# Expert tiles of a mixture of experts: another order of transposes, and products that wait for one half of their operand at a time

## The reference

```python
for e in range(N_EXPERTS):
    h = jax.nn.silu(jnp.dot(xf, w_gate[e])) * jnp.dot(xf, w_up[e])
    y = y + combine[:, e:e + 1] * jnp.dot(h, w_down[e], preferred_element_type=jnp.float32)
```

## Time and profile before

| | |
|---|---|
| runs, us | 1010.88, 1011.61, 1014.06 |
| span of the profiled execution, first to last instruction, us | 1005.1 |
| around that span, against the median, us | 6.5 |
| PE busy, share of the span | 919.4 us, 91% |
| DVE busy | 616.7 us, 61% |
| ACT busy | 534.2 us, 53% |
| the expert tiles, first product of tile 0 to last product of tile 22 | 548.8 to 973.0 us |

### The profile page before, as it was taken

The page is one execution under the profiler, slowest core; times in us unless marked ns, Lnnn a source line. Parts: engine busy times, 40 slices in busy tenths (PEclk is TensorE's granted clock), DMA queues, the critical chain, the costliest instruction groups (busy, mean ns, idle before and its releaser), DMA issues.

```text
span 1005.1 us, 15974 instructions
## 1 busy us (share of the span) xinstructions
PE 919.4 (91%) x4959; PEld 744.9 (74%) x4960; DVE 616.7 (61%) x1182; ACT 534.2 (53%) x1008; POOL 177.8 (18%) x260
## 2 busy tenths in 40 slices
PE   5899999899989999989973999999999999999982
PEld 5777888687877788867742788888888888888850
DVE  5443644655744573465698989989456494564684
ACT  4343565542445565554343878877446584464460
POOL 4300002001000011100011234435222232221301
PEclk9998999989999999989975999999999999999996
DMA  8740114116342352310755999999868697674524
GB/s 252 120 108 22 42 43 130 61 43 201 115 104 84 112 183 54 116 42 22 281 215 171 352 362 394 389 374 392 275 203 260 197 342 228 218 248 116 150 107 193
DMA packets 95119, 183.95 MB, mean 183 GB/s; under 512 B 24064, under 2 KB 52975, under 8 KB 95072
## 3 DMA queue, kind: packets, MB, share of 16 engines
q1 hardware_dynamic: 80496, 137.91, 38.3%
q0 software_dynamic: 14144, 43.88, 16.4%
q10 hardware_dynamic: 432, 1.57, 0.4%
HBM read 159.85 MB, written 28.70 MB: 188 GB/s over the span
## 4 chain that ended last, share of the span: by engine, by line
PE 41%; DVE 15%; issue 6%; DMA 4%; ACT 3%; DVEq 1%; SPq 0%; ACTq 0%; POOL 0%; POOLq 0%
PE O L2009 9%; PE C L1728 7%; PE C L1730 7%; PE C L1729 7%; DVE split_main L1594 6%; PE O L1909 3%; PE T L1962 2%; PE S L1763 2%; PE T L1884 2%; PE S L1969 1%; PE T L1792 1%; DMA mixing<-in_w_out 1%; DMA mixing<-acc_dram 1%; ACT split_main L1092 1%; DVE mixing L1675 1%
## 5 line engine op out<-in xcount | busy, mean ns | idle before, releaser
L1594 DVE TENSOR_TENSOR split_main<-mixing,split_main 128x1024 fp32r<-128x1024 f32 x188 | 217.7, 1221 | 35.0 <-ACT split_main L1092 32.3
L1092 ACT CAST split_main<-mixing 128x1024 fp32r<-128x1024 f32 x188 | 186.4, 1050 | 17.2 <-PE C L1730 7.1
L1728 PE MATMUL C<-split_main,split_aux 128*128 128x512 f32 x368 | 143.9, 391 | 1.3 <-DVE split_aux L1600 1.3
L1730 PE MATMUL C<-split_main,split_aux 128*128 128x512 f32 x368 | 143.9, 391 | 0.0
L1729 PE MATMUL C<-split_main,split_aux 128*128 128x512 f32 x368 | 143.6, 390 | 0.0
L1728 PE MATMUL C<-split_main 128*128 128x512 f32 (+1 forms) x320 | 130.4, 407 | 3.5 <-DVE split_main L1434 3.0
L2009 PE MATMUL O<-split_main,split_aux 128*128 128x512 f32 x552 | 132.7, 396 | 0.0
L1729 PE MATMUL C<-split_main 128*128 128x512 f32 (+1 forms) x320 | 121.6, 380 | 0.0
L1730 PE MATMUL C<-split_main 128*128 128x512 f32 (+1 forms) x320 | 121.4, 379 | 0.0
L2009 PEld LDWEIGHTS O<-split_main,split_aux 128*128 128x128 f32 x552 | 100.2, 188 | 23.4 <-DVE split_aux L1615 4.7
L1728 PEld LDWEIGHTS C<-split_main,split_aux 128*128 128x128 f32 x368 | 69.5, 189 | 15.9 <-issue 1.5
(11 more groups left out here) (341 smaller groups left out, 1435.3 us busy)
## 6 DMA issues: line engine op xcount, KB each, us to landing
mixing<-in_w_down SPq DMA_DIRECT2D x64, 512.0 KB, 8.2
mixing<-in_w_gate SPq DMA_DIRECT2D x64, 512.0 KB, 9.1
mixing<-in_w_up SPq DMA_DIRECT2D x64, 512.0 KB, 6.1
mixing<-in_w_in SPq DMA_DIRECT2D x20, 512.0 KB, 3.8
mixing<-in_w_out SPq DMA_DIRECT2D x16, 512.0 KB, 4.1
mixing<-in_w_mem_kv SPq DMA_DIRECT2D x8, 512.0 KB, 6.1
mixing<-in_w_in SPq DMA_DIRECT2D x16, 256.0 KB, 3.7
x_dram<-x_nat POOLq DMA_DIRECT2D x8, 512.0 KB, 2.9
```

Source lines behind the costliest of these rows:

```text
L1092: nc.scalar.copy(wu[0][:, w, :], raw[:, w, :]).then_inc(unit_hi, 1)
L1594: nc.vector.tensor_tensor(wu[1][:, w, :], raw[:, w, :], wu[0][:, w, :].bitcast(F32), ALU.subtract).then_inc(unit_lo, 1)
L1728: ins = nc.tensor.matmul(out_ap, st[0], mvg[0], start=first, stop=False)
L1730: ins = nc.tensor.matmul(out_ap, st[1], mvg[0], start=False, stop=last)
```

## The change

In the first step of a tile, each unit's six products are issued as four with high halves of the rows, then two with low halves. PE waits for the high halves (`xgT_hi`) ahead of the tile, and for the low halves only ahead of the first product that reads them, the fifth. The transposes go in the order 4 row, 1 hidden, 4 row, 3 hidden. In the third step the units f = 0 and f = 1 wait for the high half of their part first and for the low half ahead of the fifth product; f = 2 and f = 3, which read the same part as f = 1, wait for neither. The products themselves are the same 72, and so are all other engines' programs.

```diff
                 with pe.Fori(lo, hi) as j:
-                    pe.wait_ge(xgT_lo, j + 1)
+                    pe.wait_ge(xgT_hi, j + 1)
                     for w in range(KD):
                         unit_wait(e, w)
-                        for k in range(2 * (w % 4), 2 * (w % 4) + 2):
-                            ins = three(Cb[w // 4][:, :], [xgT[0][:, k, :], xgT[1][:, k, :]],
-                                        [wu[b_][:, w, (k % 2) * 512:(k % 2 + 1) * 512] for b_ in range(2)],
-                                        k == 0, k == KD - 1)
+                        half, ks = Cb[w // 4][:, :], (2 * (w % 4), 2 * (w % 4) + 1)
+                        for part in range(2):
+                            for k in ks:
+                                nc.tensor.matmul(half, xgT[0][:, k, :], wu[part][:, w, (k % 2) * 512:(k % 2 + 1) * 512],
+                                                 start=(k == 0 and part == 0), stop=False)
+                        if w == 0:
+                            pe.wait_ge(xgT_lo, j + 1)
+                        for k in ks:
+                            ins = nc.tensor.matmul(half, xgT[1][:, k, :], wu[0][:, w, (k % 2) * 512:(k % 2 + 1) * 512],
+                                                   start=False, stop=(k == KD - 1))
                         ins.then_inc(units_used, 1)
-                    transpose_rows(j + 1, 0, 2)
+                    transpose_rows(j + 1, 0, 4)
                     transpose_h(j, 0)
-                    transpose_rows(j + 1, 2, KD)
+                    transpose_rows(j + 1, 4, KD)
                     transpose_h(j, 1)
                     pe.wait_ge(y_half[0], j + 1)
                     pe.wait_ge(y_half[1], j + 1)
                     for f in range(KF):
                         unit_wait(e, KD + f)
-                        pe.wait_ge(hT_lo, j * 2 + (f > 0) + 1)
                         st = [hT[0][:, f, :], hT[1][:, f, :]]
+                        if f < 2:
+                            pe.wait_ge(hT_hi, j * 2 + 2 + f + 1)
                         for a_, b_ in ((0, 0), (0, 1), (1, 0)):
+                            if a_ == 1 and f < 2:
+                                pe.wait_ge(hT_lo, j * 2 + f + 1)
                             for half in range(2):
```

## The result

The changed kernel took 1005.46 us (median of 18 runs) where the kernel before took 1010.47 (18 runs), 5.0 us less. Four of the 18 runs were disturbed, 1011.70 to 2756.90 us, and the comparisons leave such runs out: then the ratio is 0.9933, 95% interval 0.9908 to 0.9957, a gain of 6.8 us (4.3 to 9.3). Run twice more for this study, the same kernel gave 0.9971 (0.9948 to 0.9994) and 0.9958 (0.9925 to 0.9991). The mean of the three is 0.9954, some 4.7 us; the forecast was 5.0 of 1011.61, a ratio of 0.9951. All intervals hold the forecast's ratio, but the working has to be looked at apart from the sum, since the profiles show terms that were too large and others that were too small.

What follows compares the result with a forecast made beforehand. PE's own sequence was taken to set the pace, DVE nearly as slow. Tiles 0 to 7 give 1.14, 8 to 19 3.36, tiles 20 and 22 0.24 each: 5.0 us, to 1006.6 us; range 1004.3 to 1009.7.

Steps and rivals of the forecast that it cites:

- the waits for low halves ahead of the tile and at f = 0: PE's low-half waits: said to cost nothing from tile 1 on; tile 0's 1.29 us also worth nothing.
- row transposes ahead of the first hidden one: Two more row transposes fill PE's wait ahead of the first hidden transpose: 0.24 us a tile gained.
- The wait for hidden part 1: Down products at f = 1 no longer wait for the low half: 0.04 us a tile, between 0 and 0.15.
- More waits: One wait more in each tile on PE, three now between products: taken to cost 0.
- the rival of costly waits: Three waits between products cost 0.05 us each, 0.15 a tile; gain only 1.9, time 1009.7 us; chance 0.12.
- that of no effect: DVE sets the pace, or the hole reopens at the second hidden part; time 1011.6 us; chance 0.05.
- Products at a longer step: Rival: alternating stationary operands make 48 products a tile take 0.24 us each, not 0.227; time 1019 us; chance 0.03.
- DMA in tiles 1 to 7: Full DMA engines limit one-tile experts: tile 7's hidden part 0 comes at most about 0.86 us sooner.
- The rows are waiting in SBUF already: Gathered rows are ready for the two earlier row transposes, as PE shows no idle time ahead of row transposes.
- The clock falls in tile 0: Rival: PE's earlier start lengthens idling to 2.95 us, the clock falls, about 1.5 us lost; 1008.1 us; chance 0.04.
- The end: Tile 20's rows, a load and DVE's work set the end: gain kept to tile 20's transposes, tile 21's lost.
- tile 22's 0.24: In tile 22 DVE gets ACT's copy of hidden part 1 sooner: 0.24 us gained.

Runs made afterwards that it cites:

- the run with less weight: Changed kernel, but from the third expert on only half of each gate unit is loaded, a sixth less weight to move; one run, 1005.34 us.
- the early gather: Changed kernel with POOL issuing the next gather right behind the scatter, not behind the scatter's landing; ratio 0.9926 to the kernel before.
- the filled kernel: Changed kernel with twenty unused identity transposes in tile 0, ahead of its first hidden transpose, where PE idles; ratio 0.9915, repeated 0.9959.

## Why the prediction was right and where it was wrong

**The sum.** Right in size: on the way to tile 22 the changed kernel's second and third profiles gain 4.8 and 4.9 us of 407.4. The forecast's terms up to there are 1.14 + 3.36 + 2 x 0.28 = 5.06, with tile 21's gain, which it did not expect to keep. The first comparison's 6.8 us are more than the way accounts for. Since the start alone moves by 8 us between profiles of programs that are the same up to it, much of the rest can be chance, but how much was not resolved beyond the two repeats.

**The step that failed: "the waits for low halves ahead of the tile and at f = 0" cost nothing.** I argued with the rows' low halves alone and passed over hidden part 0's. In the kernel before this wait was hidden: the down products of tile 3 began at 619.09, 1.67 us after the first row transpose, and the low half was there just before, at 618.63 + 0.29 = 618.92:

```profile
618.63 0.29 DVE L1615 TENSOR_TENSOR split_aux<-S,split_aux 128x128 fp32r<-128x128 f32 x1 [0.25 <-ACT split_aux L1245]
```

Two transposes less in between make it the next wait, and the split at f = 0, put at nothing, is worth 0.11 us a tile, 2.3 us in 21 tiles. So "row transposes ahead of the first hidden one", priced at 0.24, is 0.11 by itself, and 0.22 with the split. The wait for hidden part 1, taken at 0.04 out of a span of 0 to 0.15, is 0.06 to 0.08: that is the term that makes a tile 0.30 us shorter where 0.28 were forecast, 0.4 us in 21 tiles. The total came out because the change had both parts, which was luck as far as the argument goes: for the order alone the same argument gave 0.24, and 0.11 came.

**More waits** cost nothing that shows: tiles at 17.87 us with one wait more, so the rival of costly waits fell, and that of no effect with it. By the Trainium skill ("Advanced Engine Details and Errata", Miscellaneous Facts; 50 to 100 ns a semaphore read) 1.2 to 2.3 us were to be lost, as an estimate. The step of 0.227 us through the split products does not show it, and the measurement decides for this place. **Products at a longer step** fell with the same row.

**DMA in tiles 1 to 7** was the right mechanism at the right place: hidden part 0 of tile 7, behind two casts that wait for loads. Its size was not to be had from one profile. Measured from the first row transposes, tile 7's hidden part 0 comes 146.3 us on before, 145.9 in the second profile of the changed kernel and 144.5 in the third: a gain of 0.4 and 1.8 where 0.86 was forecast. Four variants of it whose clock did not fall and whose rows were not late up to there lie from 145.5 to 146.4. That it is the loads, their landings show, in the run with less weight above.

**"The rows are waiting in SBUF already"** was true of the kernel before, whose PE did not idle ahead of row transposes, and wrong as a reserve. Behind the gather lies a chain that the forecast left out: scatter, its landing, POOL's small operations, gather. In the one-tile stretch gathers landed 0.5 to 1.7 us ahead of their transposes before, and 0.1 to 0.5 in the second profile of the changed kernel. Where POOL's operation ahead of the first scatter takes 5.6 to 7.7 us the rows of tile 2 are 3.3 to 4 us late (three profiles without the early gather). In these tile 7 waits for nothing: late rows and late loads are not added but take turns.

**"The clock falls in tile 0"** had a chance of 0.04 and came true in one of three profiles of the changed kernel, at a higher price than the 1.5 us of the forecast: tile 1 began 9.13 us after hidden part 0 where 6.46 are due. But its cause as put, PE's earlier start, is refuted. PE did start tile 0 earlier, 3.65 us after the first row transposes in place of 4.52, by 0.87 and not by 1.29; yet the kernel before had a hole of 3.14 us too, and the kernel that waits for both halves one of 2.91. The Trainium skill's warning of idle gaps ("TensorE: Matmul & The Clock Gate", "Why this matters for your kernels") is borne out in part: the granted clock fell in three of the eight profiles with a hole of 2.9 to 3.4 us and in none of the six with 1.0 to 1.9.

**The end**: the gain of 4.8 and 4.9 us at tile 22's start is 3.9 to 4.5 at its hidden part 0, where 4.74 were forecast (958.59 - 541.34 = 417.25 in the second profile and 417.62 in the third, against 421.76 in the earlier trace rows and 421.5 in the other profile of the kernel before): tile 21's gain is lost, as forecast. What comes behind varies by 3.5 us between the two profiles of the kernel before (53.4 and 56.9 us from tile 22's start to the end), so tile 22's 0.24 can't be seen.

## What to carry to other kernels

Where a hole is filled by moving work, look for the next wait at the new place: here the second half of the operand stood 0.11 us behind, and only both edits together gave the whole. A chain with slack in one profile (gather behind scatter behind a landing) is not free when a tile gets shorter; starting the gather ahead of the landing took it out, at no price seen. A change of half a per cent is judged by stretches that begin and end inside the changed part, by several profiles and not by two spans, and by runs compared at the same granted clock. A wait that is gone in an experiment proves its cause only if the one who waited did not come later.

## What the runs showed of the hardware

A POOL operation on one element takes 0.18 us at its fastest and mostly 0.2 to 1.1 us, at most 2.2, where it begins beside one of DVE's 128x1024 subtractions, but in five of fourteen profiles L1011, or what answers to it, took 5.6 to 7.75: four times ahead of the first scatter and three times while tile 14 ran. In two profiles of the filled kernel it began 28.98 us after the first row transposes both times, and took 0.89 us once and 7.70 the other time, beside the same twelve subtractions; the second time it ended as their run ended, at 580.8. Why it waits in one run and not in the other stays open.

The granted clock is not a function of the hole alone: 3.20 us of idle time in the same place, after the same products, left it at 1.00 in two profiles and brought it to 0.50 in a third.
